# Convolution feed-forward: the up-projection's high and low features side by side in one 512-column matmul

## What is computed

```python
def _conv_ffn(h, w_up, conv_w, conv_b, w_down):   # h (1, 256, 1024), w_up (1024, 5632), w_down (2816, 1024)
    u = h @ w_up
    u = lax.conv_general_dilated(u, conv_w[:, None, :], window_strides=(1,), padding=[(2, 0)],
                                 dimension_numbers=('NWC', 'WIO', 'NWC'),
                                 feature_group_count=2 * D_FF_2) + conv_b      # D_FF_2 = 2816, width 3
    gate, val = jnp.split(u, 2, axis=-1)
    return (jax.nn.silu(gate) * val) @ w_down

x = x + _conv_ffn(_rmsnorm(x, ffn_norm[i]), ffn_w_up[i], ffn_conv_w[i], ffn_conv_b[i], ffn_w_down[i])
```

## Time and profile before

| | |
|---|---|
| time, median of 3 runs | 1375.7 us (1374.76 to 1376.05) |
| profiled execution, first to last instruction | 1373.9 us |
| PE busy | 1340.8 us (98%) |
| DVE busy | 946.7 us (69%) |
| ACT busy | 669.7 us (49%) |
| POOL busy | 81.9 us (6%) |
| loads | 279.73 MB, mean 204 GB/s |
| granted TensorE clock, mean | 0.993 |

### The profile page before, as it was taken

The page is one execution under the profiler, slowest core; times in us unless marked ns, Lnnn a source line. Parts: engine busy times, 40 slices in busy tenths (PEclk is TensorE's granted clock), DMA queues, the critical chain, the costliest instruction groups (busy, mean ns, idle before and its releaser), DMA issues.

```text
span 1373.9 us, 19832 instructions
## 1 busy us (share of the span) xinstructions
PE 1340.8 (98%) x8344; PEld 1180.2 (86%) x8344; DVE 946.7 (69%) x1094; ACT 669.7 (49%) x872; POOL 81.9 (6%) x146
## 2 busy tenths in 40 slices
PE   6999999999999999999999999999999999999996
PEld 2797898998887899998898778999998977999996
DVE  4997887775897877555874445887776445787774
ACT  3733554433647554444534444644455455654442
POOL 0211111110111100000000000000000000000000
PEclk9999999999999999999999999999999999999999
DMA  9895498786590566554465434455554522365530
GB/s 374 351 361 196 159 337 302 300 291 224 210 357 31 199 245 248 212 184 169 157 218 192 153 127 153 180 196 190 187 187 147 215 106 92 126 236 188 187 123 31
DMA packets 46696, 279.73 MB, mean 204 GB/s; under 512 B 5328, under 2 KB 5712, under 8 KB 19600
## 3 DMA queue, kind: packets, MB, share of 16 engines
q1 hardware_dynamic: 33696, 231.57, 45.9%
q0 software_dynamic: 12912, 46.90, 9.1%
HBM read 277.40 MB, written 1.05 MB: 203 GB/s over the span
## 4 chain that ended last, share of the span: by engine, by line
PE 90%; DVE 5%; ACT 1%; DMA 1%; issue 1%; SPq 1%; POOL 0%; POOLq 0%; DVEq 0%; ACTq 0%
PE ps L1771 33%; PE ps L1934 12%; PE ps L1936 12%; PE ps L1935 12%; PE ps L1831 6%; PE ps L1870 5%; PE ps L1901 1%; PE ps L2175 1%; DMA early_a<-in_ada_w 1%; DVE acc L1081 1%; PE ps L1970 1%; PE ps L1853 1%; DVE w_lo L1071 1%; PE ps L1978 1%; PE ps L2403 1%
## 5 line engine op out<-in xcount | busy, mean ns | idle before, releaser
L1071 DVE TENSOR_TENSOR w_lo<-raw,w_hi 128x2048 fp32r<-128x2048 f32 x209 | 477.4, 2289 | 162.7 <-ACT w_hi L647 162.0
L647 ACT ACTIVATE w_hi<-raw 128x2048 fp32r<-128x2048 f32 x209 | 399.0, 1912 | 185.5 <-PE ps L1771 130.9
L1934 PE MATMUL ps<-h_hi,w_hi 128*128 128x256 f32 x1344 | 381.9, 284 | 0.0
L1936 PE MATMUL ps<-h_hi,w_lo 128*128 128x256 f32 x1344 | 380.3, 283 | 0.0
L1935 PE MATMUL ps<-h_lo,w_hi 128*128 128x256 f32 x1344 | 380.3, 283 | 0.0
L1935 PEld LDWEIGHTS ps<-h_lo,w_hi 128*128 128x128 f32 x1344 | 256.3, 191 | 2.1 <-issue 0.5
L1934 PEld LDWEIGHTS ps<-h_hi,w_hi 128*128 128x128 f32 x1344 | 256.3, 191 | 2.0 <-issue 0.5
L1936 PEld LDWEIGHTS ps<-h_hi,w_lo 128*128 128x128 f32 x1344 | 256.3, 191 | 0.0
L1665 DVE SCALAR_TENSOR_TENSOR f_cv<-ps,cols,f_cv 128x254 f32<-128x254 f32 (+1 forms) x176 | 76.8, 477 | 73.0 <-ACT f_cv L983 71.4
L1771 PE MATMUL ps<-w_hi,hid_lo 128*128 128x512 f32 x344 | 106.9, 392 | 0.0
L1771 PE MATMUL ps<-w_hi,hid_hi 128*128 128x512 f32 x344 | 106.6, 391 | 0.0
(11 more groups left out here) (322 smaller groups left out, 1813.8 us busy)
## 6 DMA issues: line engine op xcount, KB each, us to landing
raw<-in_stream SPq DMA_DIRECT2D x209, 1024.0 KB, 4.9
ada<-in_ada_w POOLq DMA_DIRECT2D x80, 512.0 KB, 6.1
ada<-in_ada_w SPq DMA_DIRECT2D x4, 512.0 KB, 5.8
early_hi<-in_ada_w SPq DMA_DIRECT2D x4, 512.0 KB, 12.5
early_lo<-in_ada_w SPq DMA_DIRECT2D x4, 512.0 KB, 12.5
row<-in_gate_b POOLq DMA_DIRECT2D x4, 512.0 KB, 5.3
x<-in_x SPq DMA_DIRECT2D x1, 1024.0 KB, 8.9
early_a<-in_ada_w SPq DMA_DIRECT2D x2, 512.0 KB, 15.7
```

Of the source, the lines that this page charges most:

```text
L647: act.activation(w_hi[:, s, :], raw[:, s, :], ACT.Copy).then_inc(hi_done[s], 1)
L1071: dve.tensor_tensor(w_lo[:, s, :], raw[:, s, :], w_hi[:, s, :].bitcast(f32), ALU.subtract)\
L1934: pe.matmul(out, wh, h_hi[:, kt, :], start=kt == 0, stop=False)
L1936: last = pe.matmul(out, wl, h_hi[:, kt, :], start=False, stop=kt == KT - 1)
```

## The change

The two feature tensors become the halves of one, `h_both`, so that one matmul can stream the high and the low features of a tile, 512 columns, against the high weights. Its output fills a bank: columns 0 to 255 hold the high part's sum and columns 256 to 511 the low part's. The matmul of high features by low weights adds into the second half. That makes 2 matmuls where there were 3, and a chunk takes two banks, one for each f. Gate chunks now always use banks 4 and 5, value chunks 6 and 7.

The halves are added when they are read. ScalarE copies the second half out (`small_part`, into `f_l`), VectorE adds the first half to it (`whole`, into `f_u`), and all three taps are then read from `f_u` in SBUF. Group 0 has nothing to add: there `whole` is a copy of the turned block. TensorE waits, ahead of a chunk, for `whole` of the group before in the same banks. The value's `turn` moves into the middle of up(1,0), since it goes to bank 7 now.

```diff
-        h_hi = sb("h_hi", [P, KT, T], f32r)
-        h_lo = sb("h_lo", [P, KT, T], f32r)
+        h_both = sb("h_both", [P, 2, KT, T], f32r)
+        h_hi, h_lo = h_both[:, 0], h_both[:, 1]
...
+                def small_part(g, value):
+
+                    if g == 0:
+                        return
+                    act.wait_ge(*multiplied(ffn_chunk(c0, g, value)))
+                    act.wait_ge(fu_value if value else fu_gate, GROUPS * layer + g)
+                    act.activation(f_l[:, value, :, :], ps[:, 4 + 2 * value:6 + 2 * value, T:2 * T], ACT.Copy)\
+                        .then_inc(fl_value if value else fl_gate, 1)
+
                 def last_tap(g, value):
                     G = GROUPS * layer + g
-                    act.wait_ge(*((fc_tr, 2 * (3 + 2 * layer) + value + 1) if g == 0 else
-                                  multiplied(ffn_chunk(c0, g, value))))
+                    act.wait_ge(fu_value if value else fu_gate, G + 1)
...
                 for g in range(GROUPS):
+                    small_part(g, 0)
                     last_tap(g, 0)
                     if g < GROUPS - 1:
                         hi(c)
                     act.wait_ge(cg_dve, GROUPS * layer + g + 1)
                     act.activation(f_cv[:, g % 2, 0, :, :], f_cv[:, g % 2, 0, :, :], ACT.Silu).then_inc(fsilu, 1)
+                    small_part(g, 1)
                     last_tap(g, 1)
...
+                def whole(g, value):
+
+                    u = f_u[:, value, :, :]
+                    if g == 0:
+                        dve.wait_ge(fc_tr, 2 * (3 + 2 * layer) + value + 1)
+                        dve.tensor_copy(u.rearrange("p f t -> p (f t)"), ps[:, 6 + value, :])\
+                            .then_inc(fu_value if value else fu_gate, 1)
+                    else:
+                        dve.wait_ge(fl_value if value else fl_gate, (GROUPS - 1) * layer + g)
+                        dve.tensor_tensor(u, ps[:, 4 + 2 * value:6 + 2 * value, 0:T], f_l[:, value, :, :], ALU.add)\
+                            .then_inc(fu_value if value else fu_gate, 1)
...
-                            src = ps[:, 4 + 2 * (g % 2) + value, f * T:(f + 1) * T - back]
+                            src = f_u[:, value, f, 0:T - back]
...
+                    whole(g, 0)
                     earlier_taps(g, 0)
                     if g < GROUPS - 1:
                         lo(c)
+                    whole(g, 1)
                     earlier_taps(g, 1)
...
+            def cols_wide(c, bank, between=None):
+
+
+                s = chunk_ready(c)
+                for f in range(2):
+                    if f and between:
+                        between()
+                    for kt in range(KT):
+                        first = kt * T + f * P
+                        wh, wl = w_hi[:, s, first:first + P], w_lo[:, s, first:first + P]
+                        if kt:
+                            pe.matmul(ps[:, bank + f, T:2 * T], wl, h_hi[:, kt, :], start=False, stop=False,
+                                      skip_group_check=True)
+                        last = pe.matmul(ps[:, bank + f, :], wh, h_both[:, :, kt, :], start=kt == 0,
+                                         stop=kt == KT - 1)
...
-                def up(g, value):
-                    if g >= 2:
-
-                        pe.wait_ge(cv_dve if value else cg_dve, B + g - 1)
-                    cols_chunk(ffn_chunk(c0, g, value), 4 + 2 * (g % 2) + value)
+                def up(g, value, between=None):
+
+                    if value and g == 1:
+                        pe.wait_ge(fu_gate, B + 1)
+                    if value or g >= 2:
+                        pe.wait_ge(fu_value if value else fu_gate, B + g)
+                    cols_wide(ffn_chunk(c0, g, value), 4 + 2 * value, between)
```

More of the change, by code:

```diff
@@ L219, in build @@
         fc = at("fc", 10240, [2, TT, 256])
+        f_l = at("f_l", 9216, [2, 2, T])
+        f_u = at("f_u", 11264, [2, 2, T])
         d_q = at("d_q", 0, [TT, D])
@@ L338, in build @@
         fsilu = sem("fsilu")
+        fl_gate = sem("fl_gate")
+        fl_value = sem("fl_value")
+        fu_gate = sem("fu_gate")
+        fu_value = sem("fu_value")
         rope_q = sem("rope_q")
@@ L982, in last_tap @@
                         k = COL_CONV + ((layer * 2 + value) * FT + 2 * g + f) * (CONV + 1)
-                        last = act.activation(f_cv[:, g % 2, value, f, :],
-                                              ps[:, 4 + 2 * (g % 2) + value, f * T:(f + 1) * T],
-                                              ACT.Identity, bias=cols[:, k + 3:k + 4], scale=cols[:, k + 2:k + 3])
+                        last = act.activation(f_cv[:, g % 2, value, f, :], f_u[:, value, f, :], ACT.Identity,
+                                              bias=cols[:, k + 3:k + 4], scale=cols[:, k + 2:k + 3])
                     last.then_inc(cv_act if value else cg_act, 1)
@@ L1856, in norm_tile, with first_two @@
                         last.then_inc(tr_done, 1)
-            def first_two(c0, k, stage, i):
+            def first_two(c0, k, stage, i, turn_bank=4):
                 slots = chunk_ready(c0), chunk_ready(c0 + 1)
@@ L1874, in first_two, with turn @@
                             if second and t == 1 and kt == 1:
-                                turn(i, 0)
+                                turn(i, 0, turn_bank)
                         last.then_inc(used[s] if t else fc_mm, 1)
-            def turn(i, which):
+            def turn(i, which, bank=4):
                 pe.wait_ge(fc_done, 4 * i + 3 + which)
@@ L1883, in turn @@
                     for t in range(TT):
-                        last = pe.transpose(ps[:, 4 + which, f * T + t * P:f * T + (t + 1) * P],
+                        last = pe.transpose(ps[:, bank + which, f * T + t * P:f * T + (t + 1) * P],
                                             fc[:, which, t, f * P:(f + 1) * P], ident)
@@ L1936, in cols_chunk @@
                         last = pe.matmul(out, wl, h_hi[:, kt, :], start=False, stop=kt == KT - 1)
+                last.then_inc(used[s], 1)
+            def cols_wide(c, bank, between=None):
[11 more added lines that the diff above has]
+                                         stop=kt == KT - 1)
+                        if not kt:
+                            pe.matmul(ps[:, bank + f, T:2 * T], wl, h_hi[:, kt, :], start=False, stop=False,
+                                      skip_group_check=True)
                 last.then_inc(used[s], 1)
@@ L2343, in down @@
                          lambda k, t: hid_lo[:, g % 2, k, t * P:(t + 1) * P], g == 0, False)
-                first_two(c0, 5 + 2 * layer, stage, 3 + 2 * layer)
+                first_two(c0, 5 + 2 * layer, stage, 3 + 2 * layer, 6)
                 for g in range(1, GROUPS):
-                    up(g, 0)
-                    if g == 1:
-                        turn(3 + 2 * layer, 1)
+                    up(g, 0, (lambda: turn(3 + 2 * layer, 1, 6)) if g == 1 else None)
                     up(g, 1)
```

## The result

The changed kernel takes 1383.19 us (median of 4 runs, 1382.21 to 1384.84) against 1375.88 before, a ratio of 1.0057 with a 95% interval of 1.0045 to 1.0069. It is slower by 7.3 us, and outside the predicted range of 1372.3 to 1382.2. The profiled execution is 1381.7 us long, 7.8 more than before.

A forecast was written before the change was run, and what follows sets the result against it. TensorE bounds the kernel, with VectorE's chain a second limit at layer ends. Layer 0 +0.7 and layer 1 -0.5 sum to +0.2 us: span 1374.1, median 1375.9, 8-in-10 range 1372.3 to 1382.2.

The forecast's parts named there:

- The end of a layer: Behind up(9,0): last split 0.7 us later, TensorE waits some 4 us in layer 0; layer 0 +0.7, layer 1 -0.5.
- rival (1): In `up` chunks: wide matmul costs the two it replaces, 0.240 us, nothing saved; 1382.1 us; chance 0.17 including partial saving.
- The wide matmul: In `up` chunks: 512 columns take 0.228 us, a chunk 5.57, saving 0.185 a chunk, 3.7 a layer.
- rival (2): In `up` chunks: a matmul's fixed part is only 2.5 ns, saving 0.04 us a chunk; 1380.9 us; chance 0.06.
- The added reading: Each of 40 chunks: ScalarE copy 0.60 us, VectorE addition 0.68; taps from SBUF save 0; hidden mid-layer.
- The start of a layer: Ahead of up(1,1): TensorE waits for group 0's value copy, 0.25 us a layer.
- The middle: Middle groups: VectorE needs 15.5 us a group, TensorE 16.6, so TensorE stays the bound.
- The end's chain: From ScalarE's start after up(9,0) to the last split's end: 26.40 us instead of 22.81, 3.6 longer.
- likely case: Whole kernel: the two layers sum to +0.2 us, 1375.9, own range 1374.2 to 1377.7; chance 0.60.

The follow-up runs named there:

- fill: Changed kernel plus useless matmuls (20 in layer 0, 14 in layer 1) where TensorE waits for VectorE's last split; 1377.85 us, ratio 1.0017.
- hold4: Kernel before, plus four unused VectorE products of 1024 columns ahead of group 10's product in each layer; 1388.37 us, ratio 1.0095.
- lolate: Changed kernel with chunk 32's w_lo subtraction on VectorE moved behind group 10's gate taps; 1378.64 us, ratio 1.0028.
- hold2: Kernel before, plus two unused VectorE products of 1024 columns ahead of group 10's product in each layer; 1380.73 us, ratio 1.0040.
- three: Changed kernel with its two banks and added reading, but three matmuls of 256 columns again; 1387.1 us, ratio 1.0083.

## Why the prediction was wrong

**The step that failed** is in "The end of a layer": "TensorE arrives 20 x 0.185 - 0.25 = 3.4 earlier and waits some 4 us", priced at the length of the wait alone. The wait came, 4.7 us in layer 0 and 3.2 in layer 1. With it came a term that the sum doesn't have: the clock at its lower level when TensorE resumes, 1.95 + 3.0 = about 5 us. fill took it away without touching the data's timing, and hold4 brought it about without the change. The prediction put this term at nothing without a reason. No rival held it either; rival (1)'s time was near the measured one for a wrong reason, since nothing was wrong with the matmul's price.

The profile could have told me. In the trace of before, between 655 and 664 us, TensorE waits for VectorE twice in a short time, and the clock behind it falls. I hadn't asked for these rows, because the page of the profile shows a 9 in every slice, and I read that as the upper level throughout. The mean of 0.993 in the table ahead says otherwise: with levels of 1 and 0.5 it is an estimated 19 us at the lower one (0.007 x 1373.9 / 0.5). This is the window:

```profile
660.56:663.98 3.42, 3.28 (x15) 3.28 (x16) 1.31 (x5) 2.25 (x4) 1.61 (x2) 0.50 0.12 23
```

And this is TensorE's timeline around the two waits:

```profile
657.98 0.39 PE L1870 MATMUL ps<-w_hi,h_hi 128*128 128x256 f32 x1 [0.97 <-DVE h_lo L1131]
...
660.70 0.58 PE L1870 MATMUL ps<-w_hi,h_hi 128*128 128x256 f32 x1 [1.74 <-DVE h_lo L1131]
661.08 0.41 PE L1870 MATMUL ps<-w_lo,h_hi 128*128 128x256 f32 x1
661.29 0.41 PE L1870 MATMUL ps<-w_hi,h_lo 128*128 128x256 f32 x1
```

The rows show a clock of 0.50 and starts 0.21 apart in place of 0.12, behind waits of 0.97 and 1.74. The Trainium skill has a rule for it, in "TensorE: Matmul & The Clock Gate", section "Why this matters for your kernels": long idle gaps of TensorE between bursts of matmuls bring the clock back to its lower level. The traces agree in kind, with 0.51 behind the wait of 4.67 us. They differ in how long a gap has to be: the clock also fell, to 0.50, behind lolate's 1.9, which is shorter than the gaps that the section warns of.

**The wide matmul**: right. 0.348 us was forecast for the pair; 16.69 a group gives 5.59 a chunk, 0.349. That also decides against rival (2): 0.16 us a chunk is won, not 0.04. The 2.5 ns a matmul of the Trainium skill's "TensorE: Matmul & The Clock Gate", section "Wait — 56ns, not 53.3ns?", don't hold for the matmuls of this kernel: one of 256 columns starts 0.120 us after the last, 13 ns over its columns' time.

**The added reading**: right. The copy takes 589 ns (600), the addition 684 (680), the taps 480 (477) from SBUF. The last tap is the small miss: 594 ns where PSUM gave 560, so a pair takes 1.09 and not 1.02.

**The start of a layer**: right in kind. The wait ahead of up(1,1) was forecast at 0.25 and is about 0.4: TensorE starts it at 878.93, 0.59 after the last start of the chunk before, where 0.23 follows a 512-column matmul elsewhere.

**The middle**: right. From 872.5 to 1029.2 TensorE is busy 156.51 of 156.70 us, and the 0.19 left are the start of up(1,1).

**The end's chain**: 26.40 us was forecast. ScalarE's timeline and VectorE's in the changed kernel give its ends:

```profile
1012.63 0.60 ACT L987 ACTIVATE f_l<-ps 128x512 f32<-128x512 f32 x1 [3.61 <-PE ps L1981]
...
1029.73 1.09 ACT L997 ACTIVATE f_cv<-f_u,cols 128x256 f32<-128x256 f32 x2 [3.45 <-DVE f_u L1681]
```

```profile
1029.01 0.68 DVE L1681 TENSOR_TENSOR f_u<-ps,f_l 128x512 f32<-128x512 f32 x1
...
1033.83 0.69 DVE L1681 TENSOR_TENSOR f_u<-ps,f_l 128x512 f32<-128x512 f32 x1 [1.19 <-ACT f_l L987]
...
1038.70 0.69 DVE L1719 TENSOR_TENSOR h_both<-f_p,h_both 128x512 fp32r<-128x512 f32 x1
```

From 1012.63 to 1039.39 it is 26.76, 0.36 more, mostly the four last taps of 1.09. Against the earlier trace rows, and with the 0.9 us of the loads, up(9,0) came 2.4 earlier, not 2.9, since a chunk saves 0.16 and not 0.185 and the start of the layer costs 0.1 more. The split is thus 1.6 later than before where 0.7 was forecast, and layer 1 loses some 0.4 where it was to win 0.5. These small misses add up to about 1.8 us, and alone they would have left the time at 1377.7, the upper edge of the likely case; fill, which takes the clock's part away, measures 1377.85.

## What to carry to other kernels

Where an edit makes the bounding engine reach a dependency sooner, work out what the dependency's chain does, and price a new TensorE wait twice: its length, and the matmuls behind it at half speed. At the ends of this kernel's layers the second price came with every wait of 1.9 us and more, and not with one of 1.1. Ask for the granted clock in windows of a few microseconds behind every wait of the trace you have; 40 slices of 34 us hide it. A restructuring that adds latency to each step belongs where there is slack for it: used in groups 1 to 8 and left out in the two groups that end a layer it gains 0.35%, used in all it loses 0.57%.

## What the runs showed of the hardware

The size of the second price was not expected: about 5 us behind waits of 4.7 and 3.2 us. At the ends of the layers the clock stayed at 1.00 behind 1.1 us (hold2); it fell behind 1.9 (lolate), 2.6 (hold2), 2.7 (three) and all longer ones, up to 5.1 (hold4), with wide matmuls in the `up` chunks and without. Single waits of 1.0 us in the trace of before (ending at 161.70, 472.49 and 1148.05) leave it at 1.00 too, while the pair of 0.97 and 1.74 brings it down. What exactly decides between the two is left open.

The price isn't in proportion to the wait. Behind the waits of 1.9, 2.6 and 2.7 us the slow stretch lasted 3.4 us, behind the longer ones 6.8 to 6.9. It began while TensorE still waited in the longer cases, and only 1.2 us after it was back in lolate's layer 1. What is lost is about half of the part of the stretch in which TensorE works: 1.6 us behind hold2's 2.6, 1.95 behind the changed kernel's 4.7, but 2.8 behind lolate's 3.4.

A matmul of 512 columns and one of 256 in turns keep the sum of their own paces, 0.349 us, although the wide one reads its columns in two runs of 256, 8 KB apart.

ScalarE's 256-column instruction with scale and bias takes 594 ns with its input in SBUF and 560 with it in PSUM. VectorE's taps take 480 and 477: no difference.

Where a single trace stands before the first change varies by up to 2.4 us: the same 60 matmuls of the earlier trace rows start between 840.28 (hold2) and 842.67 (the changed kernel) in the ten traces. So ends of two traces are compared less that offset.
